# A hybrid decoder step on one core: the mixer's output projection of two prompt tiles by seven half-size products

## The reference

```
x = layer_norm(x, emb_ln)
h = x @ w_in                                # u | q | k | v | og | gates
pool_out = pooled differences of u          # 4 groups of 128 channels
mlstm_out = sigmoid(og) * norm(mLSTM(q, k, v, gates))   # 4 heads of 128
mix = concat(pool_out, mlstm_out) @ w_out   # 1024 x 1024
x = layer_norm(ALPHA * x + mix, ln1)
x = layer_norm(ALPHA * x + cross_attention(x), ln2)
x = layer_norm(ALPHA * x + moe(x), ln3)     # 16 experts, top 2 inside the top group
```

## Time and profile before

| | us |
|---|---|
| median of 3 runs | 664.78 (664.69 to 665.74) |
| the profiled execution | 665.21 |
| its span, first to last instruction | 663.5 |
| PE busy | 635.4 (96%) |
| DVE / POOL / ACT busy | 350.5 / 207.0 / 151.8 |
| mean granted TensorE clock | 0.995 of full |

### The profile page before, as it was taken

One profiled execution on the slowest core, in us unless ns is written; L12 is line 12 of the kernel. 1 busy time (PEld: TensorE's weight loads), 2 busy tenths in 40 slices (PEclk: granted clock), 3 DMA queues, 4 the chain that ended last, 5 costly groups with the idle time before them and its releaser, 6 DMA issues.

```text
span 663.5 us, 8673 instructions
## 1 busy us (share of the span) xinstructions
PE 635.4 (96%) x3244; PEld 389.2 (59%) x3244; DVE 350.5 (53%) x801; ACT 151.8 (23%) x333; POOL 207.0 (31%) x243
## 2 busy tenths in 40 slices
PE   6999999999999999999999999999999999999993
PEld 3445588887787774446888774444574444333331
DVE  0283356327457792657653865355873324244365
ACT  1113311002524230002001740221324111121144
POOL 4141010100476566411100986002243432111221
PEclk9999999999999999999999999999999999999997
DMA  8994478613344345002904987555448999999797
GB/s 300 392 329 167 143 172 225 235 42 127 100 134 157 103 161 192 17 0 81 364 0 137 337 300 275 208 206 191 175 161 346 413 408 416 389 363 413 275 198 156
DMA packets 45811, 146.14 MB, mean 220 GB/s; under 512 B 5738, under 2 KB 6058, under 8 KB 41663
## 3 DMA queue, kind: packets, MB, share of 16 engines
q1 hardware_dynamic: 31847, 108.55, 43.6%
q0 software_dynamic: 11744, 32.24, 17.2%
q10 hardware_dynamic: 2176, 4.76, 1.9%
HBM read 130.34 MB, written 20.33 MB: 227 GB/s over the span
## 4 chain that ended last, share of the span: by engine, by line
PE 81%; DMA 9%; DVE 4%; issue 2%; ACT 1%; POOL 1%; ACTq 0%; DVEq 0%; POOLq 0%
PE ps L606 15%; PE ps L753 14%; PE ps L515 9%; PE ps L481 8%; PE ps L1093 7%; PE ps L1113 4%; PE ps L604 4%; DMA P<-x_d,smp 3%; DMA xn<-y_d 2%; PE ps L854 2%; PE ps L778 2%; PE ps L662 2%; PE ps L838 1%; PE ps L677 1%; PE ps L543 1%
## 5 line engine op out<-in xcount | busy, mean ns | idle before, releaser
L753 PE MATMUL ps<-wring,P 128*128 128x512 f32 x224 | 99.2, 596 | 0.0
L753 PEld LDWEIGHTS ps<-wring,P 128*128 128x128 f32 x224 | 41.6, 190 | 49.1 <-issue 49.0
L1093 PE MATMUL ps<-wring,P 128*32 128x512 f32 (+1 forms) x288 | 63.6, 593 | 0.9 <-DVE P L2355 0.9
L1779 DVE SCALAR_TENSOR_TENSOR P<-ps,P 128x264 f32<-128x264 f32 (+1 forms) x70 | 28.8, 427 | 60.9 <-PE ps L606 44.2
L515 PE MATMUL ps<-wring,P 128*128 128x512 f32 x128 | 57.9, 610 | 1.0 <-DVE P L1734 0.8
L481 PE MATMUL ps<-xT,wring 128*128 128x312 f32 (+1 forms) x256 | 56.8, 383 | 0.0
L2522 POOL TENSOR_SCALAR rstd<-agg 128x1 f32<-128x1 f32 (+1 forms) x15 | 16.8, 1120 | 114.7 <-DVE agg L1719 114.6
L481 PEld LDWEIGHTS ps<-xT,wring 128*128 128x128 f32 x256 | 46.6, 190 | 9.3
L2355 DVE COPY P<-ps 128x512 f32<-128x512 f32 x11 | 7.6, 692 | 74.5 <-PE ps L1074 74.5
L515 PEld LDWEIGHTS ps<-wring,P 128*128 128x128 f32 x128 | 24.6, 196 | 31.0 <-issue 30.8
L1093 PEld LDWEIGHTS ps<-wring,P 128*32 128x32 f32 (+1 forms) x288 | 21.6, 128 | 35.0 <-issue 34.9
(11 more groups left out here) (445 smaller groups left out, 1104.0 us busy)
## 6 DMA issues: line engine op xcount, KB each, us to landing
wring<-in_w_in SPq DMA_DIRECT2D x5, 2048.0 KB, 9.8
...
wring<-in_ca_wv SPq DMA_DIRECT2D x2, 2048.0 KB, 20.8
```

What stands on the lines that cost most here:

```text
L753: last = mm(bk[:, :], src[:, k, START[t]:START[t] + TR], w[:, k, :], start=(k == 0), stop=(k == KC - 1))
L1093: last = mm(GU[p % 2][lo:lo + m, :].rearrange("p (g f) -> p g f", g=2), xgT[:, p % 3, k, lo:lo + m], gu[s][:, :, k, :], start=(k == 0), st ...
L1779: V.scalar_tensor_tensor(dst, src, scale, part, ALU.mult, ALU.add).then_inc(part_added, 1)
```

## The change

With the rows of tiles 0 and 1 as A, its left half the pooling groups and its right half the heads, and `w_out` in four quarters B, the eight quarter products of the 2 x 2 block product are replaced by seven. A quarter product is four matrix products of 128x512. The sums of A are made by DVE (`mixed_sums`, in the columns of `uT`), named by number: s5 = A21 - A22, s6 = s5 - A11, s3 = s6 + A12, s7 = A11 - A21. The sums of B are w5 = B11 + B12, w6 = w5 + B22, w7 = B12 + B22, w4 = w6 + B21. The products are, in PE's order: first A11 B11, second A12 B21, fifth s5 w5, third s3 B22, sixth s6 w6, seventh s7 w7, fourth A22 w4.

For w5, w6, w7 and w4, SP loads a quarter of 1024 KB each (into the columns of `kT`, the first half of ring slot 2, and the columns of `qT` and `vn`), and POOL issues a DMA that adds a second operand to it: from `w_out` in memory for w5 and w7, from SBUF for w6 and w4. The semaphore `wsum_made` counts them: P (w5), T2 (w6), T3 (w7), T4 (w4); a wait for T4 waits for all. The seven results go to `MBANK` and the DVE ring; ACT copies the first and the fifth to SBUF, and DVE combines them, tile 0 after the sixth, tile 1 after the seventh and fourth. Tiles 2 and 4 and the samples are computed as before. The load of wq0, whose slot w6 uses, now waits for T4 and for the sixth product. DVE takes head 3 before the products of state 6 instead of after them, and waits for `gb` only before the normalisation.

```diff
         for name in ("wq0", "wq1"):
             u2[name] = [wide(20046), wide(20046 + WIDE)]
+        block_at = lambda lo: view(lo, 2048, "p (k c) -> p k c", k=4)
+        wo_sums = {5: block_at(4224), 6: wring[:, 2, 0:4, :], 7: block_at(2144), 4: block_at(8384)}
+        mixed = lambda t, hf: mixT[:, 4 * hf:4 * hf + 4, START[t]:START[t] + TR]
+        mixed_sums = {p: view(512 * i, 512, "p (k c) -> p k c", k=4) for i, p in enumerate((5, 6, 3, 7))}
...
+        P_MADE, T2_MADE, T3_MADE, T4_MADE = 16, 32, 48, 64
@@ PE
-            pe.wait_ge(dve_free, at["heads", 2])
-
-            head_bank = bank_d()
...
-            rows_project(1, WO, mixT)
+            def mixed_product(bank, x, w, done, order=range(4), ready=None):
+
+                for k in order:
+                    if ready:
+                        pe.wait_ge(*ready[k])
+                    last = mm(bank[:, :], x[:, k, :], w[:, k, :], start=(k == order[0]), stop=(k == order[-1]))
+                last.then_inc(done, 1)
+
+            use_block("wo0")
+            copied = {g: (act_free, at["pool"] - 6 + 2 * i) for i, g in enumerate((2, 3, 1, 0))}
+            mixed_product(MBANK[0], mixed(0, 0), wo0[:, 0:4], act_full, (2, 3, 1, 0), copied)
...
+            transpose_heads(3, bank_d())
...
+            mixed_product(MBANK[1], mixed(0, 1), wo0[:, 4:8], dve_full, ready=turned)
+            pe.wait_ge(xsum_done, MIXED + 1)
+            pe.wait_ge(wsum_made, P_MADE)
+            pe.wait_ge(act_free, at["first"])
+            mixed_product(MBANK[0], mixed_sums[5], wo_sums[5], act_full)
...
+            mixed_product(MBANK[1], mixed_sums[3], wo1[:, 4:8], dve_full)
+            pe.wait_ge(wsum_made, T2_MADE)
+            mixed_product(bank_d(), mixed_sums[6], wo_sums[6], dve_full)
+            used[BI["u"]] = (dve_full, nd[0])
+            pe.wait_ge(xsum_done, MIXED + 4)
+            pe.wait_ge(wsum_made, T4_MADE)
+            mixed_product(bank_d(), mixed_sums[7], wo_sums[7], dve_full)
+            mixed_product(bank_d(), mixed(1, 1), wo_sums[4], dve_full)
             transpose_x(0, x1_ready)
@@ SP
-            for i in range(3, BI["wc0"] + 1):
+            for i in range(3, BI["wq0"]):
+                block_load(i)
+            low, high = [[w[:, 0:4], w[:, 4:8]] for w in (BLOCKS[BI["wo0"]][1], BLOCKS[BI["wo1"]][1])]
+            sp.wait_ge(dve_full, at["keys", 3])
+            sp.dma_start(wo_sums[5], low[0]).then_inc(piece_in[0], 16)
+            sp.wait_ge(act_full, at["u", 0])
+            sp.dma_start(wo_sums[6], high[1]).then_inc(piece_in[1], 16)
+            sp.wait_ge(dve_full, at["state", 3])
+            sp.dma_start(wo_sums[7], high[0]).then_inc(piece_in[2], 16)
+            sp.dma_start(wo_sums[4], low[1]).then_inc(piece_in[2], 16)
+            sp.wait_ge(wsum_made, T4_MADE)
+            for i in range(BI["wq0"], BI["wc0"] + 1):
                 block_load(i)
@@ ACT
+            copy_part(first_part, MBANK[0])
+            copy_part(fifth_part, MBANK[0])
@@ DVE
             head_norm2(3)
-            carried(6)
             take_heads(3)
+            V.tensor_tensor(s[5], mixed(1, 0), mixed(1, 1), ALU.subtract).then_inc(xsum_done, 1)
...
+            V.tensor_tensor(x, x, product_of(MBANK[1]), ALU.add).then_inc(dve_free, 1)
+            dve.wait_ge(dve_free, nf[0])
+            statistics(0, 0)
+            carried(6)
...
+            V.tensor_tensor(sum_part, product_of(), first_part, ALU.add).then_inc(dve_free, 1)
+            dve.wait_ge(dve_free, nf[0])
+            link(V.tensor_tensor(x, x, sum_part, ALU.subtract))
             dve.wait_ge(gb_in, 32)
-            residual(0, x1_ready)
+            norm(0, x1_ready, first_known=True)
             carried(7)
-            residual(1, x1_ready)
+            V.tensor_tensor(all_part, product_of(), sum_part, ALU.add).then_inc(dve_free, 1)
...
+            norm(1, x1_ready, first_known=True, last=0)
@@ POOL
             state_out(2)
             update_state(4)
+            pool.wait_ge(piece_in[0], 32)
+            pool.dma_start(wo_sums[5], high[0], accum_op=ALU.add).then_inc(wsum_made, 16)
             update_state(5)
             window_sums()
+            pool.wait_ge(piece_in[1], 32)
+            pool.wait_ge(wsum_made, P_MADE)
+            pool.dma_start(wo_sums[6], wo_sums[5], accum_op=ALU.add).then_inc(wsum_made, 16)
             load_state(6)
             head_rstd(3, TR, NQT)
+            pool.wait_ge(piece_in[2], 48)
+            pool.wait_ge(wsum_made, T2_MADE)
+            pool.dma_start(wo_sums[7], high[1], accum_op=ALU.add).then_inc(wsum_made, 16)
+            pool.dma_start(wo_sums[4], wo_sums[6], accum_op=ALU.add).then_inc(wsum_made, 16)
             state_out(3)
             update_state(6)
```

78 lines of the change are left out of this document (57 added, 21 removed).

## The result

The changed kernel takes 684.3 us (median of 5 runs, 681.28 to 685.12), the kernel before beside it 665.34 (664.69 to 666.71): a ratio of 1.0255, 95% interval 1.0224 to 1.0286. The forecast was 677.1 with a range of 665.5 to 688, so the direction and the range held and the size was 7 us short. The profiled execution of the changed kernel took 681.28 us, its span is 679.4; the sum of the prediction stands against that one.

A forecast was written before the change was run, and what follows sets the result against it. PE bounds the kernel. Tile 0's turn moves +10.0 us (waits 3.0 + 3.7 + 6.7, less 3.43), plus 0.3 for tile 2's bank and 2.0 clock: 12.3 on 665.2 is 677.5, less 0.4 gives 677.1 us, range 665.5 to 688.

The forecast's parts named there:

- What bounds the kernel, and the products: PE bounds the time, so its waits add to it; 28 products of 128x512 instead of 32 save 3.43 us.
- DMA's work, 5.1 us a sum: Each 1024 KB adding transfer holds all DMA engines 5.1 us, a plain load 2.7; T4 lands at about 271.7.
- the first rival: Adding costs no more than copying: T4 at 262, total 661.4 to 664 us; chance 10%.
- The root of head 3 behind T2: On POOL, T2 waits for P and the second load, delaying head 3's root to 252.7; PE waits 3.0 us.
- The seventh product: PE ends its sixth product at 268.0 and waits 3.7 us for T4, to 271.7.
- The vectors: gb waits for state 3's stores behind T3 and T4, lands at 280.9; PE waits 6.7 us, tile 0's turn at 285.3.
- The clock: After PE's last, longer wait its clock is at half speed for a while: 2 us, between nothing and 4.8.
- Edits that cost nothing: wq0's later load, ACT's two copies and DVE's four token differences add no time.
- The four differences of the tokens: On DVE, 0.7 us each, during PE's second and fifth product; if late, the fifth would wait under 1 us.

The follow-up runs named there:

- e3: The kernel before with the change's four loads, four sums, their waits and later wq0 load, but its old 32 products, which read no sums: 683.42 us, ratio 1.0252.
- e1: The change with its four adding transfers made plain copies, all loads, waits and orders kept: 676.93 us, ratio 1.0159 to the kernel before.
- e4: The change with state 3's two stores issued ahead of T3 and T4 on POOL: 677.03 us, ratio 1.0163 to the kernel before.
- e5: The change with products that nobody reads (3, 3 and 9) put into PE's three waits: 680.73 us, ratio 1.0208 to the kernel before.
- e6: e2 with gb's loads issued right behind state 3's stores, ahead of update_state(6), on POOL: 663.94 us, ratio 0.9957 to the kernel before.
- e2: The change without its loads and sums, four products reading plain quarters of w_out instead: 667.84 us, ratio 1.0021 to the kernel before.
- e10: The change with sums by POOL and DVE (w5 at 226), gb earlier, head 3 turned inside the second product, its root ahead of load_state(6): 679.94 us.
- e12: The change with w5, w7 by early adding transfers, w6, w4 by DVE, e6's and e10's orders, wq0's load behind state 7's, tile 0's root ahead of stores: 663.98 us.

## Why the prediction was right, and what its sizes missed

**What bounds the kernel, and the products.** Held. Each microsecond that PE waits is in the time: 14.2 us of waits, 3.4 less of products, 3.8 of half clock (below) and 1.2 ahead of the stage make 15.8, and the span grew by 15.9; the parts are good to about half a microsecond. A product at full clock costs 3.43 us in every run. That their gain is not seen at all is also as the sum had it, since the turn of tile 0 was put at gb's landing plus 4.4 us; e3 shows it.

**DMA's work, 5.1 us a sum.** Right in kind, short by about 0.3 us (196 GB/s over T3 and T4, where 204 was taken from the earlier trace rows). T4 landed at 274.1 (261.41 + 12.7), predicted 271.7. Half of the 2.4 us lies ahead of the stage: the eight short products of head 3 in front of the pooling products start at 243.38 in the change and at 242.20 in the kernel before, but in the experiments' profiles anywhere from 241.99 to 243.45, so that goes with the run. The other 1.2 are what four sums of 0.3 more would give. The rule quoted from the Trainium skill, "DMA: Bandwidth & Descriptors", by which a sum would take 4.4 us alone, 2.4 of them for the bytes, would have brought the first rival. The trace does not agree with it for adding transfers: T3 and T4 held all engines about 5.4 us each. No sum ran alone here. e1, where they copy, moved 374 GB/s in the stretch in which the change moved 189.

**The root of head 3 behind T2.** Predicted a wait of 3.0, measured 2.88. T2 was issued at 249.98 (predicted 250.1), the root ended at 253.6 (252.7). That T2's time fits so well is in part luck. The prediction named two waits ahead of T2 and took P's landing, at 249, as the one that counts. P landed at 247.5 (issued at 237.58, 9.9 us), and POOL then stood 2.2 us more for w6's plain load, issued only at 239.53, when its ring slot came free, and landed at 249.7: the row at 249.98 names it, and so does the chain. In e1 it is the same, P at 242.9 and T2 at 247.21. So a cheaper P alone would not have brought head 3 forward.

**The seventh product.** Predicted 3.7, measured 3.19. It is a wait for T4, while the seventh product reads only w7, and T3, which makes w7, had landed at 269.1 (260.58 + 8.5), ahead of PE's need at 270.97. Both count on one semaphore. A kernel with a semaphore for each was not run; in the change the gain would have been hidden, since gb sets the turn.

**The vectors.** The term that decides held by its mechanism, and e4 shows it: the stores moved ahead alone give back 6 to 7 of the 17 to 19 us (17 by the ratio, 19 by the medians). Its sizes: gb issued at 275.11 (272.2), landed at 284.8, 9.7 us after its first issue (8.7), rows ready 4.5 us later (4.4), wait 8.12 (6.7). Tile 0's turn is at 289.38 against 285.3. The 4.1 us are the 1.2 ahead of the stage, 1.7 of T4 and the store behind it, 1.0 of gb beside wq0's load, which was the half-shared 2.7 and measured 3.7, and rounding.

**The clock.** The term of 2 us is right for the profiled run: the turn of tile 0 is 0.93 us longer than in the earlier trace rows, that of cq 0.46, tile 2's stage 0.7. (The product at 255.38 is 1.7 longer than the 3.60 of its like, but the wait for T4 would have been longer without it.) It says nothing of the median, and there the forecast is short by 3.4 us more: it took 0.4 off for the step from the profiled run to the median, and the changed kernel's other four runs stand 1.8 to 3.8 above its profiled one, at a clock 0.01 lower. Where in these runs the clock was lower no trace shows; e3's trace, at about their clock, has a fall at 508 to 517 us that costs 3.3 (see e5). By "TensorE: Matmul & The Clock Gate", Part 1, of the Trainium skill, activity must first release the gate again. The windows of 0.50 behind the first and the last wait agree; behind the second, of 3.19 us, the clock had not fallen.

**Edits that cost nothing.** wq0's load, ACT's copies: held in the change. One was wrong though nothing shows it there. "The four differences of the tokens" and tile 0's first half were costed as DVE's work alone; they also push carried(6) from 252 to 259, and with it update_state(6) and gb, by 8 us. In the change this hides behind T3 and T4. With the transfers gone it is 2.7 of the 3.9 us between e6 (663.9) and e2 (667.8), by the starts of tile 2 at 275.15 and 277.84; e2's profile also has a fall of the clock behind this stage, e6's hardly any. The prediction's first rival, "adding costs no more than copying", gave 661.4 to 664 without it and put T4 at 262; in e1 it landed at 269.0, and gb queues behind copies as well.

So the sum was 3.8 us short against the profiled run (681.28, 677.5): tile 0's turn came 4.1 later than predicted, 1.2 of that from ahead of the stage and the rest from the transfers, and what follows it cost 0.6 less than the 2.3 put down; the remainder is rounding. The other 3.4 us of the median's 7.2 lie between the profiled run and the others.

**What stays open.** Why the profiled run of the change has a higher clock than its others was not found, nor what decides whether the clock falls at 490 to 517 us. e1's profiled run is 4.6 us shorter than the change's, and the turn of tile 0 accounts for all of it; the rest of the 7.4 between the medians is not placed. And e10's reorder was never run alone, so what part of e12's gain is its own is not known.
